# Level products of a triangular inverse: the moving operand read twice, 64 columns in place of 32

## The reference, cut to what matters

```
def step(s, inp):
    r_t, w_t, k_t, v_t, kk_t, a_t = inp
    sa = jnp.einsum('bhvk,bhk->bhv', s, -kk_t)
    s = s * w_t[:, :, None, :] + sa[..., None] * (kk_t * a_t)[:, :, None, :] + v_t[..., None] * k_t[:, :, None, :]
    return s, jnp.einsum('bhvk,bhk->bhv', s, r_t)
```

## Time and profile before

| | us |
|---|---|
| median of 3 runs | 1710.3 (1709.29 to 1711.38) |
| the profiled execution, its own time | 1714.57 |
| its span, first to last instruction | 1712.8 |
| TensorE busy with matmuls | 1528.4 (89%) |
| TensorE weight loads | 979.6 (57%) |
| VectorE busy | 608.6 (36%) |
| ScalarE busy | 530.9 (31%) |
| GpSimd busy | 264.5 (15%) |
| mean granted clock of TensorE | 0.901 of full |

### The profile page before, as it was taken

One profiled execution on the slowest core, in us unless ns is written; L12 is line 12 of the kernel. 1 busy time (PEld: TensorE's weight loads), 2 busy tenths in 40 slices (PEclk: granted clock), 3 DMA queues, 4 the chain that ended last, 5 costly groups with the idle time before them and its releaser, 6 DMA issues. The chain is left out here.

```text
span 1712.8 us, 41184 instructions
## 1 busy us (share of the span) xinstructions
PE 1528.4 (89%) x17678; PEld 979.6 (57%) x17678; DVE 608.6 (36%) x1520; ACT 530.9 (31%) x1202; POOL 264.5 (15%) x260
## 2 busy tenths in 40 slices
PE   3997978978999999589999998989987879999997
PEld 1554555545555555345557777777774455555554
DVE  2003573252121112621315566555561431121116
ACT  3113453232121111300244555565541321121112
POOL 0000040010000001100055544455500020000010
PEclk8999889898999999889997778778788989999999
DMA  9324547637999999312200000000003378999992
GB/s 390 112 99 175 218 183 303 244 130 274 364 374 372 379 366 401 159 59 112 75 2 3 4 5 6 6 5 4 4 6 124 115 304 303 376 378 369 381 381 101
DMA packets 54037, 328.34 MB, mean 192 GB/s; under 512 B 6646, under 2 KB 10038, under 8 KB 18712
## 3 DMA queue, kind: packets, MB, share of 16 engines
q1 hardware_dynamic: 43632, 290.07, 44.0%
q0 software_dynamic: 5184, 18.88, 2.8%
q10 hardware_dynamic: 5096, 17.58, 2.6%
HBM read 304.35 MB, written 22.16 MB: 191 GB/s over the span
## 5 line engine op out<-in xcount | busy, mean ns | idle before, releaser
L1398 PE MATMUL ps<-ring,arena 128*64 128x256 f32 x2048 | 243.6, 386 | 6.0 <-ACT arena L1513 4.9
L1398 PEld LDWEIGHTS ps<-ring,arena 128*64 128x64 f32 x2048 | 142.1, 138 | 96.8 <-issue 35.9
L298 PE MATMUL ps<-HT,ring 128*128 128x384 f32 x544 | 181.1, 497 | 14.2 <-PEq L367 8.2
L298 PEld LDWEIGHTS ps<-HT,ring 128*128 128x128 f32 x544 | 105.6, 195 | 89.7 <-issue 20.4
L1408 PE MATMUL ps<-ring,arena 128*32 128x128 f32 x4096 | 133.4, 277 | 0.0
L1602 DVE TENSOR_TENSOR arena<-arena,ps 64x256 f32<-64x256 f32 (+1 forms) x128 | 40.6, 358 | 252.2 <-ACT arena L1519 252.2
L1434 PE MATMUL ps<-ring,arena 128*64 128x512 f32 x512 | 129.8, 605 | 0.0
L1408 PEld LDWEIGHTS ps<-ring,arena 128*32 128x32 f32 x4096 | 107.4, 111 | 26.9 <-issue 25.4
L1518 ACT ACTIVATE arena<-ps 64x256 f32<-64x256 f32 x64 | 24.2, 378 | 309.7 <-PE ps L1398 309.7
L298 PE MATMUL ps<-arena,ring 128*128 128x384 f32 x256 | 84.8, 495 | 18.8 <-DVEq L2053 18.8
L1526 ACT ACTIVATE arena<-ps 32x256 f32<-32x256 f32 x128 | 47.9, 374 | 160.3 <-PE ps L1434 159.2
(11 more groups left out here) (358 smaller groups left out, 2285.6 us busy)
## 6 DMA issues: line engine op xcount, KB each, us to landing
ring<-wstream SPq DMA_DIRECT2D x272, 1024.0 KB, 7.5
moe_rows<-arena ACTq DMA_DIRECT2D x28, 384.0 KB, 7.2
arena<-moe_tokens POOLq DMA_DIRECT2D x12, 512.0 KB, 15.5
moe_rows<-arena ACTq DMA_DIRECT2D x4, 512.0 KB
consts<-cst ACTq DMA_DIRECT2D x1, 1655.0 KB, 17.1
XT<-xT ACTq DMA_DIRECT2D x1, 1536.0 KB, 11.2
yT<-HT SPq DMA_DIRECT2D x3, 384.0 KB, 3.2
arena<-wa SPq DMA_DIRECT2D x1, 1024.0 KB, 4.7
```

The costliest lines, as they stand in the source:

```text
L298: mm = pe.matmul(bank(m % 8), w[:, k, m % 2 * P:m % 2 * P + P], rhs[:, k, :], start=k == 0, stop=k == KC - 1)
L1398: mm = pe.matmul(bank(h, 256)[HD * x:HD * x + HD], TOKE[:, k, 0:MANY], w[:, kk, x, :], start=k == 0, stop=k == KC - 1)
```

## The change

`each` lets every product of levels 1 to 4 read its 32 moving columns twice, through a broadcast dimension of 2, and writes 64 columns to PSUM, two equal copies side by side. The products of a direction then fill 384 columns of their bank in place of 192. `left_dve` reads both copies plainly where it read one copy twice; it handles 384 elements a partition as before. `right_dve` reads the first copy alone, 192 elements a partition in runs of 32 with a stride of 64. Level 5 is as it was. The number of instructions on each engine, their order and all waits stay as they were.

```
 def left_dve(dve, c, n, d):
     dve.wait_ge(s_ll, c * NLL + (2 * n - 1 + d))
-    p_ = bank(LEFT_BANKS[d], NCH * 32).rearrange("p (n j) -> p n j", j=32)
     if n == NLEV:
+        p_ = bank(LEFT_BANKS[d], NCH * 32).rearrange("p (n j) -> p n j", j=32)
         dve.tensor_copy(dn(PF)[:, d, :, 0:32], p_).then_inc(s_ls, 1)
         return
     mask = msk1(C_LEV + 2 * (n - 1) * CH, d)
     dve.tensor_tensor(dn(PF)[:, d].rearrange("p n (b j) -> p n b j", b=2),
-                      p_.unsqueeze(2).broadcast_to([P, NCH, 2, 32]),
+                      bank(LEFT_BANKS[d], NCH * HD).rearrange("p (n b j) -> p n b j", b=2, j=32),
                       mask.rearrange("p n (b j) -> p n b j", b=2), ALU.mult).then_inc(s_ls, 1)
...
-    dve_o(dve.tensor_tensor(dtc, dtc, bank(RIGHT_BANKS[d], NCH * 32), ALU.subtract))
+    once = bank(RIGHT_BANKS[d], NCH * HD).rearrange("p (n b j) -> p n b j", b=2, j=32)[:, :, 0]
+    dve_o(dve.tensor_tensor(DTC[:, d], DTC[:, d], once, ALU.subtract))
     dve.transpose(dc, dtc).then_inc(s_inv, 1)
...
 def each(pe, o, left, right, d):
     for n in range(NCH):
         for h in halves:
-            mm = pe.matmul(bank(o, 32, 32 * n)[h], dn(left)[h, d, n], right[h, d, n], start=True, stop=True)
+            mm = pe.matmul(bank(o, HD, HD * n)[h].rearrange("p (b j) -> p b j", b=2), dn(left)[h, d, n],
+                       right[h, d, n].unsqueeze(1).broadcast_to([HD, 2, 32]), start=True, stop=True)
     return mm
```

## The result

The changed kernel takes 1658.6 us (median of 4 runs, 1657.1 to 1659.4) against 1710.8 us before; the ratio is 0.969, with a 95% interval of 0.9671 to 0.9709. The forecast was 1666.4 us, in a range of 1648 to 1694.

What follows compares the result with a forecast made beforehand. TensorE at a lowered clock was taken to bound the recurrent stage. Gain 56.2 - 5.3 (columns) - 7.0 (cold time left) = 43.9 us: 1670.7 us against the profiled 1714.6, 1666.4 us for the median; range 1648 to 1694.

Steps and rivals of the forecast that it cites:

- Where the gain comes from: Recurrent stage, about 885 to 1295 us: TensorE sets the pace in two cold stretches, 23.9 us of a 51.2 us pair.
- The mask edit and the subtraction: VectorE's two edited lines: mask 550 ns before and after, subtraction about 350 ns; possible 6 us PSUM loss taken as nothing.
- GpSimd stayed covered: GpSimd's operand products for the next pair, needed by `own_pe`: 1.9 us of slack left, so no new bound.
- The second stretch: Left product of level 4 to the first step: 15.02 us shrinks to the last pair's 9.65 us, gain 5.4 us.
- The first stretch: From 995.75 to the second L1992 at 1007.76, 12.01 us: warm, it ends at 1005.5 after VectorE's mask, gain 2.3 us.
- The price of the columns: 64-wide passes cost 2.5 ns more warm, nothing cold: 264 passes on the path, 0.66 us a pair, 5.3 us in all.
- The cold time left: 3 us of a pair's 23.9 us stay cold, an eighth: 7.0 us of the 56.2 us gain lost.
- The reading of the clock: Recurrent stage: TensorE at 0.50 while busy without a break, much of it with 32-column products; wider products might hold the clock up.
- nothing for the clock: Rival: engine work counts, not what it streams; both cold stretches stay, 1712 to 1716 us; chance of slower 0.10.
- the 5.3 us: Deduction for the wider products' passes over the stage, 0.66 us a pair, taken off the 56.2 us gain.
- 43.9: Forecast gain in us over the whole kernel: 56.2 - 5.3 for columns - 7.0 for cold time left.

## Why the prediction held, and where not

**Where the gain comes from** was right: the recurrent stage, its two cold stretches, TensorE's clock. The mask edit and the subtraction cost nothing, as put; GpSimd stayed covered: its last operand product ends at 1046.36, and `own_pe` starts at 1049.18.

**The second stretch** came out as worked out from the last pair: 9.70 us, forecast 9.65 plus 0.2 for the columns of level 4.

**The first stretch** was sized too small. "Gain 2.3 us" was 3.7 us (12.01 to 8.29). VectorE's mask was indeed what the crossed products waited for, 5.05 us after the left product of level 1 where I had 5.4. The failed step is the sum behind it: I added the crossed products and the left and right products between them, 4.3 us one after the other; they took 3.24 us (1025.11 to 1028.35). That is 1.0 us, with the earlier mask 1.4 us a pair, some 11 us in all. The trace of before showed it already: from 1005.60 to 1007.76, at 2.4 GHz, its crossed products L2466 and its L2484 start in turn.

**The price of the columns** was put too high, at 0.66 us a pair. A call of 24 wide passes takes 0.75 us (1029.20 to 1029.95), 31.3 ns a pass, against 30.0 ns. With the steps' gap filled in both, a period without cold time takes 43.0 us with all products wide and 42.8 us with all narrow (and the gap at level 4 filled as well): 0.2 us, where I had 0.66. The 42.5 us of two periods with levels 3 and 4 narrow are no price of columns: each begins behind a slow inverse, so that TensorE waits 0.52 us for ScalarE's states and not 1.33.

**The cold time left**, an eighth by choice, was 20.8 of 184.3 us, a ninth. At the 1.0 us that a stretch of 3.4 us adds to a period (44.0 against 43.0) it costs about 6 us, an estimate, where I had 7.0. That was a guess that came true.

**A wait I didn't name**: with the inverse over sooner, ScalarE's copies in front of the first step come last, and give back 0.8 us a pair, 5.7 us. I had followed VectorE and GpSimd to their next consumers, not ScalarE; the last pair of the trace of before had this very gap before L2607, 1.33 us behind ScalarE's L2248, and I took only its 9.65 us:

```profile
1281.70 0.69 PE L2607 MATMUL ps<-ring,arena 128*64 128x64 f32 x16 [1.33 <-DVE ring L2409]
```

Together: the stretches as measured hold the price of the columns already, so the 5.3 us come back whole. 43.9 + 11.4 + 5.3 - 5.7 + 1 gives 56 us; the stage of the two profiled executions lost 56.3 us. The medians differ by 52.2 us, and no trace shows where the other 4 us went. So there is luck in the forecast for the median, 7.8 us off. Against the profiled executions, from which it was worked out, it was 13.6 us off (1670.7 and 1657.1), and ScalarE's wait, which it left out, cancelled part of the first stretch and the columns.

**The reading of the clock** was only half right, and that is the step that failed in kind. I read the rows as: dense work with 32 columns lets the clock down. The kernel with 32 columns and filled gaps shows 256 us at 2.4 GHz. What the runs show is two things. In the middle pairs the falls come behind two idle gaps of about 1 us (with each gap filled, its own fall goes); and with narrow products the clock stays down for 10 to 17 us afterwards, with wide ones, inside the stage, for 3.4 or 6.8 us. In the changed kernel the gap at level 4 is still there, 0.95 us, and no fall follows it in any pair.

A gap of 1 us is neither needed nor enough, though. In the first pair of the kernel with filled gaps the clock fell with no gap over 0.40 us before it. In the last pair of before, narrow products with a gap of 0.98 us at 1268.73 kept 2.4 GHz for 34.1 us, and the wait of 1.33 us at the first step was followed by no fall in a middle pair, neither in the changed kernel nor in the narrow one with filled gaps. What the engine streams around a gap counts too, so my reading held in part; which measure of it decides stays open. The rival "nothing for the clock" fell by the result. Its argument, that idleness counts, was worth more than the tenth I gave it: it is why another cure works nearly as well. Why wide products bring the clock back sooner is not shown.

## What to carry to other kernels

Look at the granted clock stretch by stretch, and at what lies in front of each fall: a 1 us wait in a stream of small products can cost 4 to 5 us behind it. There are two cheap cures: make small products wider where the output has room, or fill the gap with products that nobody reads; the first also shortens the way back from a fall. And when TensorE gets faster, walk every engine, ScalarE too, to its next deadline, best in a place of the trace where the clock is already high.

## What the runs showed that I had not expected

- TensorE at 2.4 GHz through 256 us of a stream with 384 of its passes a pair only 32 columns wide, once two gaps of 1 us were filled with 60 passes of 32 columns.
- Widening only the left products, half of the calls, is as good as widening all: 1659.6 against 1658.6 us.
- VectorE copies from SBUF to SBUF of 32x384 elements take 0.35 us each alone and up to 1.9 us beside GpSimd; as products of two operands 0.55 and up to 2.1 us.
- Crossed 64x128 products and 64x64 products in turn finish in 3.24 us where their separate calls add up to 4.3 us.
- The clock falling in a stream of 32-column products whose longest idle gap was 0.40 us, and staying up behind gaps of 1.33 us in front of products of 64 and 128 columns.
